# One written pattern for the order of plain, block and down chunks in a SwiGLU layer, and 30 block groups in place of 28

## The reference, cut to what matters

```python
def swiglu(h, w_gate, w_up, w_down):
    return (jax.nn.silu(h @ w_gate) * (h @ w_up)) @ w_down

def reference(x, ...):                       # x (1, 256, 2048), D_FF = 5632, float32
    for l in range(2):
        if l == 1: k_nope, k_pe, v = shared_mla_kv(rms_norm(x, kv_in_norm), ...)
        if l < 1:  x = x + multiscale_pool_mixer(rms_norm(x, pool_norm[l]), ...)
        else:      x = x + mla_layer_mixer(rms_norm(x, attn_norm[0]), ...)
        x = x + swiglu(rms_norm(x, ffn_norm[l]), w_gate[l], w_up[l], w_down[l])
    return rms_norm(x, final_norm)
```

## Time and profile before

| | |
|---|---|
| median of 3 runs | 1746.88 us (1745.84 to 1747.18) |
| the profiled execution | 1745.04 us, its span 1743.2 us |
| granted TensorE clock, mean | 0.999 |
| PE busy | 1721.5 us, 99% |
| DVE busy | 1403.0 us, 80% |
| ACT busy | 1151.0 us, 66% |
| POOL busy | 222.3 us, 13% |
| chain that ended last | PE 85%, DVE 11%, DMA 1% |

### The profile page before, as it was taken

How to read it: one execution, slowest core, us unless ns; L and a number is a source line. 1 busy time by engine, 2 the same in 40 slices (tenths; PEclk the granted TensorE clock), 3 DMA queues, 4 the chain that set the end, 5 groups by cost and what they waited for, 6 DMA issues and landing times.

```text
span 1743.2 us, 32496 instructions
## 1 busy us (share of the span) xinstructions
PE 1721.5 (99%) x12816; PEld 1632.9 (94%) x12816; DVE 1403.0 (80%) x1765; ACT 1151.0 (66%) x1753; POOL 222.3 (13%) x244
## 2 busy tenths in 40 slices
PE   9999999999999999999999999999999999999998
PEld 6888999999999999889999888899999999999997
DVE  5898777788877887798997779787778888878766
ACT  6656667677776676566775456576767766767753
POOL 2100000001000000364112420000000000000000
PEclk9999999999999999999999999999999999999999
DMA  6677878788888896755445457787887788879772
GB/s 227 213 235 210 255 229 256 241 246 246 246 252 245 243 302 160 248 188 161 148 139 170 156 183 225 225 257 230 251 265 222 237 253 252 243 229 267 224 250 94
DMA packets 111020, 388.81 MB, mean 223 GB/s; under 512 B 12448, under 2 KB 13856, under 8 KB 110752
## 3 DMA queue, kind: packets, MB, share of 16 engines
q1 hardware_dynamic: 94464, 327.03, 51.8%
q0 software_dynamic: 16128, 58.73, 19.4%
q10 hardware_dynamic: 288, 1.11, 0.2%
HBM read 326.01 MB, written 2.10 MB: 188 GB/s over the span
## 4 chain that ended last, share of the span: by engine, by line
PE 85%; DVE 11%; ACT 1%; DMA 1%; issue 1%; SPq 0%; DVEq 0%; ACTq 0%
PE ps L705 17%; PE ps L706 9%; PE ps L907 9%; PE ps L909 9%; PE ps L910 9%; PE ps L713 7%; PE ps L715 7%; PE ps L717 7%; DVE w_lo L1719 5%; DVE raw L1809 2%; PE ps L790 2%; PE ps L724 1%; PE ps L725 1%; PE ps L726 1%; ACT w_hi L1264 1%
## 5 line engine op out<-in xcount | busy, mean ns | idle before, releaser
L1719 DVE TENSOR_TENSOR w_lo<-raw,w_hi 128x1024 fp32r<-128x1024 f32 (+2 forms) x793 | 944.4, 1199 | 269.9 <-ACT w_hi L1264 267.3
L1264 ACT ACTIVATE w_hi<-raw 128x1024 fp32r<-128x1024 f32 (+2 forms) x794 | 816.4, 1034 | 211.5 <-PE ps L706 137.1
L705 PE MATMUL ps<-xg,w_hi 128*128 128x512 f32 x1088 | 383.6, 393 | 4.6 <-DVE w_lo L1719 4.6
L713 PE MATMUL ps<-act,w_hi 128*128 128x256 f32 x1152 | 321.9, 279 | 0.2 <-DVE w_lo L1719 0.2
L715 PE MATMUL ps<-act,w_hi 128*128 128x256 f32 x1152 | 322.0, 279 | 0.0
L717 PE MATMUL ps<-act,w_lo 128*128 128x256 f32 x1152 | 321.4, 279 | 0.0
L706 PE MATMUL ps<-xg,w_lo 128*128 128x256 f32 x1088 | 306.5, 282 | 0.0
L907 PE MATMUL ps<-w_hi,mix_hi_lo 128*128 128x256 f32 x896 | 254.4, 284 | 7.5 <-DVE w_lo L1719 7.3
L910 PE MATMUL ps<-w_hi,mix_hi_lo 128*128 128x256 f32 x896 | 251.7, 281 | 0.0
L909 PE MATMUL ps<-w_lo,mix_hi_lo 128*128 128x256 f32 x896 | 251.7, 281 | 0.0
L705 PEld LDWEIGHTS ps<-xg,w_hi 128*128 128x128 f32 x1088 | 204.3, 188 | 47.7 <-DVE w_lo L1719 7.1
(11 more groups left out here) (252 smaller groups left out, 2637.5 us busy)
## 6 DMA issues: line engine op xcount, KB each, us to landing
raw<-w_stream SPq DMA_DIRECT2D x224, 512.0 KB, 5.0
raw<-w_group SPq DMA_DIRECT2D x224, 512.0 KB, 6.4
raw<-raw POOLq DMA_DIRECT2D x112, 512.0 KB, 5.5
raw<-w_stream SPq DMA_DIRECT2D x64, 384.0 KB, 4.9
raw<-w_o SPq DMA_DIRECT2D x32, 512.0 KB, 3.3
raw<-w_down SPq DMA_DIRECT2D x28, 512.0 KB, 6.3
raw<-w_q_a SPq DMA_DIRECT2D x8, 512.0 KB, 3.2
raw<-w_kv_a SPq DMA_DIRECT2D x8, 512.0 KB, 3.3
```

Source lines behind the costliest of these rows:

```text
L705: pe.matmul(ps[:, bank, :], w_hi[:, s, j * P:(j + 1) * P], moving, start=start, stop=False)
L713: pe.matmul(dst, w_hi[:, s, j * P:(j + 1) * P], moving[:, 0:SEQ], start=False, stop=False, skip_group_check=True)
L1264: nc.scalar.activation(dst, src, ACT.Copy).then_inc(hi_ready, 1)
L1719: nc.vector.tensor_tensor(lo, src, hi.bitcast(F32), ALU.subtract).then_inc(lo_ready, 1)
```

## The change

The number of groups of stage 2 goes from 2 to 3, so a layer has 15 groups and 14 plain tiles, and 346 chunks. `evenly`, `GROUPS_FROM`, `SETTLE` and `TAIL` go; `up_order` deals the same three sequences out by a written string of 346 letters.

```diff
-STAGE_GROUPS = (0, 3, 2, 3, 3, 3)
+STAGE_GROUPS = (0, 3, 3, 3, 3, 3)
-GROUPS_FROM = 20
-SETTLE = 8
-TAIL = 8
-def evenly(a, b):
-    ...
+ORDER = (
+    "PPPPPPPPPPPPPPPPPPPPSSPPPPPSSPPSPSSSPPPSPSSSSSDSDSDSDSSDSSSSDSSSSDSSDSSD"
+    "SDSSDSSSSSSDSDSDSSSSDSSSSSSSSSSDSDSDSPSSSSSSSSPSSSDSDSSSSDSSSSDSDSSDSSDS"
+    "SDSDSDSSDSSSSDSSSSDSDSSDPSDPSSSDSSSPSSDPSPDSSDDSSPDDSSDSSDDSSDSSSPSPSSDS"
+    "SSSSDDSSSSDDSSDSSSDSPDSSSPSDSDSSDSSSSDDSSPDSSSSDSSSDSSPSSSSPDSSDPSDSSSDS"
+    "SSSDPDSSSSDDPSDSSSSDSSSSSDDSSSSDSSDSDSSPDDSSSSSSSSSDDPPPPP"
+)
 def up_order():
-    seven = [[("S", sum(STAGE_GROUPS[:s]) + g, r, c) ...
-    ...
+    turn = {
+        "S": iter([("S", g, r, c) for g in range(LAYER_GROUPS) for r in PRODUCTS for c in range(2)]),
+        "P": iter([("P", p, c) for p in range(LAYER_PLAIN) for c in range(4)]),
+        "D": iter([("D", s, d) for s in range(STAGES - 1) for d in range(DT)]),
+    }
+    return [next(turn[kind]) for kind in ORDER]
```

More of the change, by code:

```diff
@@ L117 @@
 READS = {"P1": "W11", "P5": "W11", "P6": "W11", "P2": "W21", "P7": "W12", "P3": "W22", "P4": "W21"}
-def evenly(a, b):
[L122 to L128, removed]
-def up_order():
[L133 to L146, removed]
+ORDER = (
+    "PPPPPPPPPPPPPPPPPPPPSSPPPPPSSPPSPSSSPPPSPSSSSSDSDSDSDSSDSSSSDSSSSDSSDSSD"
+    "SDSSDSSSSSSDSDSDSSSSDSSSSSSSSSSDSDSDSPSSSSSSSSPSSSDSDSSSSDSSSSDSDSSDSSDS"
+    "SDSDSDSSDSSSSDSSSSDSDSSDPSDPSSSDSSSPSSDPSPDSSDDSSPDDSSDSSDDSSDSSSPSPSSDS"
+    "SSSSDDSSSDDSSDSSSDSPDSSSPSDSDSSSDSSSSDDSSPDSSSSDSSSDSSPSSSSPDSSDPSDSSSDS"
+    "SSSDPDSSSSDDPSDSSSSDSSSSSDDSSSSDSSDSDSSPDDSSSSSSSSSDDPPPPP"
+)
+def up_order():
+    turn = {
[4 more added lines that the diff above has]
+    return [next(turn[kind]) for kind in ORDER]
 UP_ORDER = up_order()
```

## The result

| | before | after |
|---|---|---|
| median of 14 runs each | 1745.74 us (1744.76 to 1747.87) | 1749.53 us (1745.96 to 1752.28) |
| the profiled execution, its span | 1745.04, 1743.2 | 1749.49, 1747.6 |
| layer 0's list of chunks | 39.59 to 717.77: 678.2 | 39.99 to 718.17: 678.2 |
| layer 1's list | 1013.25 to 1687.82: 674.6 | 1015.34 to 1693.10: 677.8 |
| between the lists | 295.5 | 297.2 |

The ratio is 1.0022 [1.0014, 1.0029]: the changed kernel is slower by 0.2%, where 0.3% faster was forecast (1741.1), and the time is above the range given. The four differences of stretches, 0 + 3.2 + 1.7 - 0.9, and 0.4 ahead of the first list, are the 4.4 us between the two spans. The 1741.1 stood on the median of three runs before, 1746.88; of 14 runs it is 1745.74. The change itself was forecast at -5.8 us and is +3.8, so 9.6 us have to be explained and not 8.4.

What follows compares the result with a forecast made beforehand. PE was taken as the bound, busy 1721.5 of 1743.2 us, plus its few waits, mostly for DVE. Per layer -1.93 - 5.7 + 1.8 + 2.9 = -2.9, twice -5.8, giving 1741.1 us; range 1735.0 to 1747.5.

Steps and rivals of the forecast that it cites:

- part 1: PE's work, 28 groups to 30: 8 plain chunks traded for 14 block chunks and one turn, -1.93 us a layer.
- part 2: Middle of the pattern: PE's lateness where DVE is late falls from 8.7 to 3.0 us, -5.7 a layer.
- part 3: First block chunks, now side by side at places 20 and 21: PE waits for DVE's splits, +1.8 us a layer.
- part 4: End of each list: first down tiles wait for the last group's low part, queued late on DVE, +2.9 us a layer.
- the rule for a late low part: Lateness of chunk j + 4: 1.35 plus DVE's work minus PE's chunks between; it left 0.8 us a layer in the middle.
- the 2.2 added for what the rule misses and for landings: Middle of the pattern: 1.1 us for earlier misses and 1.1 for late weight copies, giving 3.0 a layer.
- Its test on the kernel before: Late-chunk sums on the old middle gave 7.6 us where 8.7 was read; 4.6 against 4.8 to 5.0 at group 1.
- the forecast's own sign: Layer 1's list of chunks: 668.8 us expected; 672 or more would mean wrong on the whole.
- Rival (d): PE's clock falls behind the 2.9 us gaps at the list ends: +9.7, in all +3.9, 1750.8 us; chance 0.03.
- Rival (c): Middle: DVE's deficit only moves, PE gains nothing from the letters between; +5.6 with all 8.7 kept, 1752.5 us; chance 0.07.
- Rival (a): List ends: the wait is hidden because the last group's low part is made earlier; -11.6, 1735.3 us; chance 0.13.
- Rival (b): Middle: weight landings come a microsecond or two late, keeping 5 of its 8.7 us; -1.8, 1745.1 us; chance 0.20.

Runs made afterwards that it cites:

- experiment 4: The kernel before with one number changed, three groups in stage 2 instead of two, order still dealt by `evenly`: 1749.44 us, ratio 1.002.
- experiment 1: The changed kernel with DVE writing a turned group's low part (`group_act`) ahead of the plain tile's sums: 1740.34 us, ratio 0.9966.
- experiment 6: The changed kernel with the plain letter at place 292 moved to the string's end, so six plain chunks end the list: 1741.17 us, ratio 0.9971.
- Experiment 8: The changed kernel with the loads of the first group's W22 and W21 sorted behind one more streamed load: 1744.61 us, ratio 0.9989.
- experiment 10: The changed kernel with only a new head (single block chunks between single plain ones), the wait at each list's end kept: 1739.23 us, ratio 0.9957.
- experiment 11: The changed kernel with new head and six-plain-chunk tail, but 28 groups, 14 block chunks taken out evenly over places 94 to 160: 1729.4 us, 0.9911.
- experiment 9: The changed kernel with new head and six-plain-chunk tail, but 28 groups, group 5's block chunks taken out where they stood: 1746.42 us, ratio 1.0004.
- 2: The changed kernel with the first 44 letters of the pattern as in the kernel before: 1747.43 us, ratio 1.001.
- 3: The changed kernel with `group_act` ahead of the plain tile's sums on DVE and the old first 44 letters: 1739.6 us, ratio 0.9962.

## Why the prediction was wrong

| us, layer 0 / layer 1 | forecast | measured | |
|---|---|---|---|
| part 1, work | -1.93 | -1.93 | from experiment 4: its lists, less its lateness |
| part 2, middle, left of 8.7 / 8.4 | 3.0 | 3.2 / 3.9 | read in the timeline |
| part 3, head, for 1.2 / 1.0 | 3.0 / 2.7 | 5.8 / 6.1 | 1.0 of layer 1's is the clock |
| early plain chunks | 0 | 0 / 1.1 | layer 1's chunks 11 and 15 |
| part 4, end | 2.9 | 3.2 / 3.2 | 3.05 as idle time |
| clock behind the end | 0 | 1.7 / 0 | |

**Parts 1 and 4 held, part 2 held as a number.** The middle gives back 5.5 and 4.5 us where 5.7 was forecast. But the rule for a late low part (four chunks back, plus DVE's work between) had left 0.8 us a layer by itself, and 3.2 and 3.9 were measured. That the forecast of 3.0 came near is owed to the 2.2 added for what the rule misses and for landings, which is partly luck. Group 3's start is clean as forecast and group 9's 0.3 for 0.4, but group 5's, put at 0.3, takes 1.0 and 2.8, and groups 4 and 7, which the rule left out, take 0.8 and 1.1 in layer 0. Its test on the kernel before was misread in one place: where group 1 begins, given as 4.8 to 5.0 late, the timeline reads 4.6 in layer 0 and 4.2 in layer 1 without the turn, so the rule's 4.6 was not low there. The wait at the end was named with its line, its count and its chain, and the timeline has the same chain, 0.3 longer from start to start. DVE ends `group_act` at 717.80, 2.84 behind 714.96 (2.9 was forecast), and PE starts 0.37 later, which the forecast left out. Experiments 1 and 6 show that the wait is no more than an order: 8 to 9 of 1749 us, with what goes along with it, hang on where one instruction, or one letter, stands.

**Part 3 is the step that failed**, at the sentence "Behind it five plain chunks let DVE recover". DVE did recover. What didn't was the stream of loads: the forecast followed PE, ACT and DVE through the new head and left SP out. SP waits in program order too; while DVE was 2.9 us behind, nothing was loaded for four us, and the bunch that followed made chunks 26 and 29 late by 2.9 (layer 0) and 2.2 us more. Experiment 8 shows it, by moving loads alone, and narrows it: with the same pause but one streamed load ahead of the four quarters (2 MB), both are on time. Layer 0's head cost 2.8 us more than forecast, layer 1's 3.4, with 1.0 of the clock at chunk 23. By the forecast's own sign, a list of 672 us or more in layer 1, it was wrong on the whole: the list took 677.8.

**Rival (d), the clock, got 0.03 and happened.** The argument was that the rows at the end of the kernel show 1.00 for four us after PE's last matmul, and 2.9 is less. But one fall seen once gives no such bound: here the clock fell behind idle times of 3.05, 2.9 and even 1.89 us, and behind equal ones it didn't. Its size had been put at 9.7, all 14 tiles behind both gaps; measured are 1.7 of layer 0's, and 2.0 (experiment 6) or 1.4 (experiment 10) above the gaps' own 6.4 in the medians. The Trainium skill (TensorE: Matmul & The Clock Gate, "Why this matters for your kernels") advises against idle gaps between bursts of matmuls, and the traces here agree in part: in all profiles PE stood for 1.9 us or more in 22 places in front of more matmuls, and behind 14 of them the clock fell. It was cited in the prediction and weighed too little.

**The sum.** Forecast -5.8 in two layers. To that come 6.2 for the heads, 1.1 for the early chunks, 1.4 for the middle (0.2, and 1.2 in layer 1, which started from 8.4), 0.6 for the end, 1.7 for the clock, and -0.9 behind layer 1's list, where before's 0.8 us wait for x is gone: +4.3. With the 0.4 ahead of the first list that is 4.7, for the 4.4 between the spans; the 0.3 are hundredths of many chunks. Rival (c) had the sign right for the wrong reason: DVE's deficit didn't stay in the middle. Rival (a) is refuted by the row of waits. Rival (b) was right in kind, late landings, and its sign came (ACT's waits for a group's quarters grew from 4.4 to 14.4 us), but it placed them at the joins of groups.

**The fifteenth group** was taken in the forecast for a gain of 1.93 a layer. Under `evenly` it costs 3.5 us net (experiment 4, against 1745.9), and under the mended pattern a kernel without it is 2.0 us faster (11), which is little above the spread of runs. PE's work is saved and given back as lateness around its start, since DVE has too few plain and down chunks to catch up in.

What stays open: why the clock falls behind one gap and not behind another of the same length; what the rest of experiment 1's gain is; whether experiment 9's wait is the order of loads; why chunk 11 of layer 1 was 0.7 late in the changed kernel; and how much of the 0.8 us between experiments 1 and 6 is more than noise. No experiment takes the waits away and keeps the clock low, so the clock's share rests on the windows and on the runs of experiment 10.

## What to carry to other kernels

When an edit makes one engine late, follow the load queue through the same stretch as well: a queue that issues in order turns a delay of 3 us into a pause and a bunch, and if loads that are wanted later stand first in the bunch, it is paid some chunks on, where the engines look innocent. After any change of order look first at the ends of a stage: a product that waits for all its inputs needs other work in front of it, as long as the chain behind the last of them, and the order on the engine that ends this chain counts as much as the order on PE. Price a new PE gap of 2 to 3 us at its own length and up to three us more for the clock (1.0 to 2.8 here, where it fell), and count saved matmul work only once the engine that feeds PE has been summed over the same stretch.

## What the runs showed of the hardware

The granted clock went to 0.5 for 3 to 7 us after PE had stood still, at 1.0 to 2.8 us each time, but not every time. In the profiles it fell behind 4 of 8 idle times of 1.9 us (changed kernel, 1, 6, 8), 2 of 4 of 2.5 to 2.9 (2, 3), 6 of 8 of 3.0 to 3.1 (changed kernel, 2, 8, 10) and both of 5.4 and 6.3 (9), and in no other place between a kernel's first matmul and its last. One program has runs with a mean of 1.000 and of 0.997 to 0.998, which are 3 to 5 us apart (experiment 10), and a kernel with such gaps spreads over 6.3 us (changed kernel, 14 runs) where one without spreads over 3.1 (before, 14 runs) or 1.9 (experiment 11, 5 runs). The median landing of a group's quarter rose from 6.4 to 7.0 us and of the copy inside SBUF from 5.5 to 5.9, with 7% more of both.
